# Reordering the engine programs of a two-way RWKV scan: in-chunk products behind the transitions, the decay diagonals moved, fewer filler products

## The reference, cut to what matters

```python
y = _wkv7_scan(rh, w_f, kh, vh, kk, ah)
y = y + flip(_wkv7_scan(flip(rh), flip(w_b), flip(kh), flip(vh), flip(kk), flip(ah)))
...
bonus = jnp.sum(rh * kh * r_k.astype(f32), axis=-1, keepdims=True) * vh
```

## Time and profile before

| | us |
|---|---|
| median of 3 runs | 4020.55 |
| range of the runs | 4017.84 to 4028.12 |
| the profiled execution, whole | 4013.84 |
| its span | 4012.1 |
| the scan in it (1735 to 2137 us) | 402 |
| one half turn of it, late in the scan | 22.7 |

### The profile page before, as it was taken

One profiled execution on the slowest core, in us unless ns is written; L12 is line 12 of the kernel. 1 busy time (PEld: TensorE's weight loads), 2 busy tenths in 40 slices (PEclk: granted clock), 3 DMA queues, 4 the chain that ended last, 5 costly groups with the idle time before them and its releaser, 6 DMA issues. The chain is left out here.

```text
span 4012.1 us, 63663 instructions
## 1 busy us (share of the span) xinstructions
PE 3873.1 (97%) x26819; PEld 3058.8 (76%) x26819; DVE 2264.1 (56%) x3174; ACT 1349.8 (34%) x2256; POOL 1346.7 (34%) x554
## 2 busy tenths in 40 slices
PE   8999999999999999988889999999999999999998
PEld 6866788867678887577776788778777787877886
DVE  5756567487667755567774776455550626252034
ACT  3356333243223333445553433322232111103222
POOL 1011444443234441000001444355554343654442
PEclk9999999999999999999999999999999999999999
DMA  5311222322122222531112222222212112222221
GB/s 178 129 62 41 87 105 84 111 107 108 60 84 87 101 105 106 187 118 50 46 40 87 84 105 89 89 81 84 84 63 78 62 66 87 92 105 84 87 102 63
DMA packets 43518, 359.86 MB, mean 90 GB/s; under 512 B 4323, under 2 KB 4707, under 8 KB 23948
## 3 DMA queue, kind: packets, MB, share of 16 engines
q1 hardware_dynamic: 43276, 356.35, 24.6%
HBM read 333.79 MB, written 22.28 MB: 89 GB/s over the span
## 5 line engine op out<-in xcount | busy, mean ns | idle before, releaser
L364 POOL TENSOR_TENSOR ffn_weights_low<-weight_ring,ffn_weights_high 128x2048 fp32r<-128x2048 f32 x128 | 591.7, 4622 | 785.1 <-ACT ffn_weights_high L469 784.3
L211 PE MATMUL banks<-ffn_in_high,ffn_weights_low 128*128 128x512 f32 x2048 | 800.2, 391 | 10.8 <-POOL ffn_weights_low L364 8.8
L213 PE MATMUL banks<-ffn_in_high,ffn_weights_high 128*128 128x512 f32 x2048 | 797.6, 389 | 0.0
L212 PE MATMUL banks<-ffn_in_low,ffn_weights_high 128*128 128x512 f32 x2048 | 797.4, 389 | 0.0
L211 PEld LDWEIGHTS banks<-ffn_in_high,ffn_weights_low 128*128 128x128 f32 x2048 | 384.8, 188 | 97.3 <-POOL ffn_weights_low L364 11.3
L212 PEld LDWEIGHTS banks<-ffn_in_low,ffn_weights_high 128*128 128x128 f32 x2048 | 384.9, 188 | 80.5 <-issue 0.7
L213 PEld LDWEIGHTS banks<-ffn_in_high,ffn_weights_high 128*128 128x128 f32 x2048 | 384.8, 188 | 80.0
L469 ACT ACTIVATE ffn_weights_high<-weight_ring 128x2048 fp32r<-128x2048 f32 x128 | 245.2, 1915 | 558.2 <-PE banks L213 558.2
L4034 POOL TENSOR_TENSOR third_weights_low<-weight_ring,third_weights_high 128x1024 fp32r<-128x1024 f32 x144 | 360.3, 2502 | 11.6
L623 DVE SCALAR_TENSOR_TENSOR ffn_gate<-ffn_up,columns_sb,ffn_gate 128x511 f32<-128x511 f32 (+1 forms) x132 | 273.2, 2069 | 160.7 <-ACT ffn_value L513 160.7
L4032 POOL CAST third_weights_high<-weight_ring 128x1024 fp32r<-128x1024 f32 x144 | 158.4, 1100 | 511.6 <-PE banks L213 482.7
(11 more groups left out here) (671 smaller groups left out, 7536.5 us busy)
## 6 DMA issues: line engine op xcount, KB each, us to landing
weight_ring<-weights SPq DMA_DIRECT2D x143, 2048.0 KB, 7.7
scan_in<-rwkv_operands SPq DMA_DIRECT2D x7, 1280.0 KB, 5.8
rwkv_operands<-rwin_staged SPq DMA_DIRECT2D x23, 256.0 KB, 2.2
scan_in<-rwkv_operands SPq DMA_DIRECT2D x8, 512.0 KB, 4.3
bias_tiles<-bias_rows SPq DMA_DIRECT2D x8, 448.0 KB, 8.7
residual<-x SPq DMA_DIRECT2D x4, 512.0 KB, 6.5
hyena_u_x_T<-decay SPq DMA_DIRECT2D x2, 1024.0 KB, 8.0
rwkv_residual<-residual SPq DMA_DIRECT2D x1, 2048.0 KB, 7.1
```

The lines of the kernel that those rows point to most:

```text
L211: pe.matmul(out, w[1], x[0], start=start, stop=False, skip_group_check=True)
L212: pe.matmul(out, w[0], x[1], start=False, stop=False, skip_group_check=True)
L213: return pe.matmul(out, w[0], x[0], start=False, stop=stop, skip_group_check=True)
L364: pool.tensor_tensor(parts[1], landed, parts[0].bitcast(F32), ALU.subtract).then_inc(S["split"], 1)
```

## The change

No arithmetic is added or taken away but the filler products. `within` is split into two halves (part 0 takes two of the four column groups, part 1 the other two). On PE, part 0 goes ahead of `state_step(u - 1, 1)`, right behind `transitions` and `values_carried`; part 1 behind that step. `bonus_sums` goes from behind `values_carried` to the place between `turned(u - 1, 5)` and `solved(u - 1)`. `key_rows(u + 1)` goes ahead of `carried(u, 4)`, and `past(u - 1)` behind it. The filler products go from 3 to 2 in a forward half turn, from 5 to 4 in a backward one (other counts in the first and the last), to other places: 87 become 72.

On ACT, `decay_diagonals` goes from the end of its own half turn to the start of the next pass, behind `values(u)` and ahead of `turned(u - 1, 5)`; `transitions` goes ahead of `values_carried`, and the four `decays` come earlier. On DVE, `bonus_times_value` goes ahead of `substituted`, `read` ahead of `crossed(u, 3)`, `keys` ahead of `carried(u, 3)`, `written` and `bonus_product` behind it, `past` ahead of `rows_read`, and `crossed(u, 5)` ahead of `tails`.

```diff
-            def within(u):
+            def within(u, part):
...
-                if u + 1 < HALVES:
+                if part == 0 and u + 1 < HALVES:
                     need(u + 1, "spread_done", 1)
-                for j in range(JT):
+                for j in range(part * JT // 2, (part + 1) * JT // 2):
...
-                mm.then_inc(S["own_sum"], 1)
+                if part == 1:
+                    mm.then_inc(S["own_sum"], 1)
...
                 turned(u - 1, 5)
+                bonus_sums(u)
                 if last:
                     unread(u, 1, 2)
                 solved(u - 1)
...
                 transitions(u - 1)
                 values_carried(u)
-                bonus_sums(u)
-                if u == 0 or last or u % 2 == BWD:
+                if 0 < u < HALVES and u % 2 == BWD:
+                    unread(u, 1, 2)
+                if u == 0 or last:
                     unread(u, 1, 8 if u == 0 else 3)
-                else:
-                    unread(u, 1)
+                within(u - 1, 0)
                 state_step(u - 1, 1)
-                within(u - 1)
+                within(u - 1, 1)
                 if last:
                     unread(u, 3)
                 state_step(u - 1, 2)
+                if 0 < u < HALVES:
+                    unread(u, 3)
                 turned(u, 2)
-                if last:
+                if u == 0 or last:
                     unread(u, 3)
                 state_step(u - 1, 3)
-                if u % 2 == FWD:
-                    unread(u, 3)
                 crossed(u, 3)
-                if last or u % 2 == BWD:
+                if u == 0 or last:
                     unread(u, 3)
                 state_step(u - 1, 4)
+                if 0 < u < HALVES:
+                    unread(u, 3)
                 carried(u, 3)
-                if last:
+                if u == 0 or last:
                     unread(u, 3)
                 state_step(u - 1, 5)
-                unread(u, 3)
                 turned(u, 3)
...
                 crossed(u, 4)
+                if u == 0:
+                    unread(u, 3)
+                key_rows(u + 1)
+                carried(u, 4)
                 past(u - 1)
-                carried(u, 4)
-                key_rows(u + 1)
                 turned(u, 4)
                 crossed(u, 5)
...
                 values(u)
+                decay_diagonals(u - 1)
                 turned(u - 1, 5)
                 tail_rows(u)
                 solved(u - 1)
                 factors(u)
-                values_carried(u)
-                transitions(u - 1)
                 if u >= 0:
                     decays(u + 1, 0)
+                    decays(u + 1, 1)
+                transitions(u - 1)
+                values_carried(u)
                 state_step(u - 1, 1)
                 if u >= 0:
-                    decays(u + 1, 1)
+                    decays(u + 1, 2)
+                written(u - 1)
                 state_step(u - 1, 2)
-                written(u - 1)
+                if u >= 0:
+                    decays(u + 1, 3)
                 turned(u, 2)
...
                 state_step(u - 1, 6)
-                decay_diagonals(u)
                 key_rows(u + 1)
                 turned(u, 4)
...
                 masked(u, 1)
+                bonus_times_value(u)
                 substituted(u, range(SUB - 1))
                 blocks_placed(u)
+                read(u - 1)
+                crossed(u, 3)
+                keys(u + 1)
+                carried(u, 3)
+                written(u - 1)
                 bonus_product(u + 1)
-                bonus_times_value(u)
-                written(u - 1)
-                crossed(u, 3)
-                read(u - 1)
-                carried(u, 3)
-                keys(u + 1)
                 crossed(u, 4)
                 sides(u + 1)
                 carried(u, 4)
+                past(u - 1)
                 rows_read(u + 1)
-                past(u - 1)
+                crossed(u, 5)
                 tails(u + 1)
-                crossed(u, 5)
```

More of the change, by code:

```diff
@@ L3519, in _ @@
                 factors(u)
-                values_carried(u)
-                transitions(u - 1)
                 if u >= 0:
                     decays(u + 1, 0)
+                    decays(u + 1, 1)
+                transitions(u - 1)
+                values_carried(u)
                 state_step(u - 1, 1)
                 if u >= 0:
-                    decays(u + 1, 1)
+                    decays(u + 1, 2)
+                written(u - 1)
                 state_step(u - 1, 2)
-                written(u - 1)
+                if u >= 0:
+                    decays(u + 1, 3)
                 turned(u, 2)
                 state_step(u - 1, 3)
-                if u >= 0:
-                    decays(u + 1, 2)
-                    decays(u + 1, 3)
                 state_step(u - 1, 4)
@@ L3696, in read @@
                 R = AR[:, d, :, 1, :].rearrange("p j (q t) -> p q j t", q=2)
-                if d == FWD:
-                    need(u, "own_done", 1)
+                need(u, "own_done" if d == FWD else "own_sum", 1)
                 dve.tensor_tensor(R, R, both(d)[:, :, 256:512].rearrange("p q (j t) -> p q j t", j=JT), ALU.add).then_inc(S["read_done"], 1)
```

## The result

The changed kernel takes **4031.71 us** (median; 4023.01 to 4037.55), the kernel before beside it 4019.73 (4013.11 to 4028.12). The ratio is 1.0030, with a 95% interval of 1.0022 to 1.0038: 12 us more, 9 to 15. The profiled execution of the changed kernel has a span of 4029.9 us (4031.6 in all), 17.8 more than the one of before, which lay 5.9 us under its kernel's median. So a sum made from the two traces comes out at 17.6 for the scan, and some 6 us of it belong to the two executions and not to the kernels.

What follows compares the result with a forecast made beforehand. No engine bounds the scan by its sum; handoffs between three in-order programs do. Seven forward half turns at +0.9 and eight backward at -0.2 give +4.7, with the ends +4: 4024 us, range 4009 to 4040.

Steps and rivals of the forecast that it cites:

- my own signs: Marks of a wrong forecast: forward first parts under 14 us, second part half a microsecond from 8.7, over ten half-clock stretches.
- Backward first part: Backward half turn, first grams to turning of X: 0.2 us shorter, 13.6 after 13.80, mainly from PE's first-state wait going.
- The 0.1 for splitting `within`: PE's run of `within`: splitting it breaks the overlap of its column groups once, for about 0.1 us.
- Forward, late Y: Forward half turn: eight diagonals between `values` and Y delay Y by 1.9 us and, with `tails`, all behind by 2.0.
- the rival that X ends the first part: X, not PE, ends the first part, so splitting `within` saves nothing; sum +6, 4026 us; chance 0.08.
- Forward, -1.1 regained: Forward half turn, PE from `values_carried` to turning of X: 2.28 us instead of 3.34; with late Y, first part +0.9.
- Second part: Turning of X to next first grams: about 8.7 us, taken as a change of 0, ends -0.3 and +0.3.
- The clock rival: Clock falls at the wait before `solved` in most half turns: 12 more at 1.2 us, +14, above 4038; chance 0.18.
- The waits go and nothing comes back: Rival: diagonals fit somewhere, PE's waits vanish in all parts; -15 us, 4006; chance 0.14.

Runs made afterwards that it cites:

- e2: Changed kernel with only ACT's `decay_diagonals` put back at the end of its own half turn; 4020.20 us, ratio 1.0001 to the kernel before.
- e6: Changed kernel with diagonals back at the half turn's end, `bonus_sums` back behind `values_carried`, `bonus_times_value` behind `blocks_placed`; 4009.18 us, ratio 0.9976 to the kernel before.
- e7: e6 with the filler product behind state step 5 put back, in all half turns but the first and last; 4012.28 us, ratio 0.9979 to the kernel before.
- e3: Kernel before with one edit: PE's `bonus_sums` ahead of `solved` instead of behind `values_carried`; 4017.88 us, ratio 0.9995 to the kernel before.
- e4: Changed kernel with diagonals back at the half turn's end and bonus store held until level 3 is added to X; 4019.47 us, ratio 0.9993 to the kernel before.

## Why the prediction came out as it did

I forecast 4024, +4 us, and it became +12: inside the range and on the right side, at the very edge of what I had called no change. That it lay inside is in part luck: the range reached up to 4040 for falls of the clock that did not come as I had them, and what filled it, 15 us of stops, stands in no term of the sum. Two of my own signs came out against me: the forward first part is 17.16 and not 14.9, and the forward second part, 9.61 on average, is more than half a microsecond from 8.7. By its steps:

**Backward first part: right.** I wrote 13.6; the half turns without any "issue" stop have 13.45. The wait before the first state step is gone. The 0.1 for splitting `within` does not show: at u = 13 both halves and the two state steps take 1.79 us, against 1.78 in the earlier trace rows. The means with stops fell from 14.64 to 14.11.

**Forward, late Y: right in size.** 2.40 us behind `values` as written, `solved` 1.99 later (6.26 against 4.27) where I had 2.0, and well over a microsecond of wait before it. X is placed 14.11 us behind the first grams, 2.12 later than before (I had 2.3), and never held PE in these seven half turns, so the rival that X ends the first part is out. The two runs around it bracket the price: +16 for the diagonals alone, with three falls of the clock in it, and -12 for undoing them; seven half turns at 1.9 to 2.0 are 13 to 14.

**Forward, -1.1 regained: this is the step that failed.** I took the 1.78 us of the backward half turn and 0.1 for the split, added one filler, and so let PE run from `values_carried` to the turning of X in 2.28 us. By its work it does: in half turn u = 12, from the start of `solved` to the turning, 10.15 us less the stop of 1.68 are 8.47, against 9.70 in the earlier trace rows, so 1.23 would have been regained. But the stop is there: 2.39 us on average (16.74 / 7). The first part is 17.16 and not 14.9. I took a run of PE to be as short as its products, though the earlier trace rows already showed a stop of 1.82 us that no engine caused, and I used it only for the clock. The missing row was the spacing of such stops, and the missing term is the time in which a dense run of small products can get its instructions. Moving the bonus ahead of `solved` thinned out what had covered it: with the diagonals in their old place, bonus early against bonus late is 0 against -10 us (e2, e6; the store moves with it).

**Second part: near my 0 as a change, by two errors.** The means rise by 0.27 forward and 0.08 backward, inside the ends of 0.3. But undisturbed forward second parts are 8.34 (u = 6, 10, 14), better than the 8.7 that I worked out, and the other four have half clock and 10.32 to 10.94. The waits of 0.40 before `turned`, which I had covered by "PE waits there for X anyhow", are the price of the filler that left, and they cost nothing (e7).

**In sum**, over the scans of the two traces: forward first parts +4.2 of work and late Y and +15.0 of stops (16.74 - 1.73); forward second parts +1.9; backward first parts -4.2, second +0.6; first half turn +1.0; the end -0.8. But for rounding that is the 17.6 between these two executions, of which 12 stands in the medians.

**The clock rival: its place and number were wrong, its price a little low.** Twelve more half-clock stretches were to stand at the wait before `solved`. There are four in the scan, after three, and none stands there. The stretch of the wait and the next one, in half turn u = 12 of the changed kernel:

```profile
2044.90:2048.30 3.40, 1.76 (x15) 0.96 (x18) 3.26 (x7) 3.36 (x12) 0.00 (x0) 1.00 0.00 0
2048.30:2051.70 3.40, 3.40 (x99) 3.15 (x92) 1.76 (x4) 2.23 (x6) 0.00 (x0) 1.00 0.03 5
```

PE was busy for 1.76 us of 3.40 and kept 2.4 GHz. With the diagonals moved alone there is no bonus in that wait, and it is 2.72 us long. There the clock did fall right behind it, in three of seven forward half turns (u = 8, 10, 14); u = 10:

```profile
1994.29:1997.69 3.40, 0.68 (x10) 0.47 (x8) 3.26 (x7) 3.15 (x11) 0.00 (x0) 1.00 0.00 0
1997.69:2001.09 3.40, 3.40 (x64) 3.40 (x66) 0.01 (x1) 1.88 (x4) 0.00 (x0) 0.50 0.02 5
```

That the bonus in the wait kept the clock up is what these two kernels suggest; they differ in more than the bonus, and no run isolates it. By the rule of the Trainium skill that the prediction weighed ("TensorE: Matmul & The Clock Gate", Part 4, PE-mode transpose) the stretch with the turning in it should look emptier still; it kept its clock in all seven half turns, and no run here separates transposes from products. All four stretches of the changed kernel begin in a forward second part instead, behind the stop in `within`; the first of them, with the stretch ahead of it:

```profile
1806.33:1809.73 3.40, 2.10 (x58) 1.72 (x58) 0.69 (x1) 1.41 (x4) 0.00 (x0) 1.00 0.00 0
1809.73:1813.13 3.40, 2.93 (x45) 2.27 (x45) 2.00 (x4) 0.50 (x3) 0.00 (x0) 0.50 0.02 5
```

These second parts are 2.0 to 2.6 us longer than the 8.34 of the others. The 2.6 belong to u = 2, where the half clock lasts for 6.83 us, twice as long as in the others. Less the other stops and waits that stand in them alone ("issue" 0.57 and 0.53, ACT's state 0.74), the other three cost 1.3 to 1.6 each; I had priced a stretch at 1.2. The link between stop and clock is seen, not isolated: the three half turns without a fall had stops of 2.70, 2.75 and 1.72 too.

**"The waits go and nothing comes back"** failed in its condition, ACT's order, as argued. Without the diagonals' move and the bonus's, the rest of the change does give 10 us, of the 15 that this rival had named.

**Open:** what passes in the 1.1 to 1.6 us between the end of a packet and PE's next instruction, which instruction asks for the next block, and whether a stop brings down the clock behind it. No run here tried it.

## What to carry to other kernels

Work that nobody needs yet must not be placed in an in-order engine's list between a late input and the copy that another engine waits for, even when that engine is idle for most of the time: look on which side of the wait the idle time lies. Before filling or removing a wait of PE in a run of small products, look for "issue" stops in its timeline and count all of PE's instructions between them, waits included; where they lie on a grid, removed waits and removed work can come back as stops. In such a run, independent work in a few large products was free here (e6), and was better kept there than moved into a wait elsewhere.

## What the hardware showed

PE's program arrives in blocks, and a dense run of small fp32 products is faster than they come. Each of these products counts as two instructions, weight load and product; 256 of PE's instructions go with one packet of 16 KB (84 packets in the scan for 84.0 such blocks), and at the long stops PE stood for 0.98 to 3.08 us and went on 1.1 to 1.6 us after the packet had ended. The Trainium skill, in "Runtime: NRT & Kernel Launch", section "Instruction fetch mechanics", says that instructions are refilled in blocks of 16 KiB, 256 instructions, and that the cost of crossing a border is mostly hidden. The traces agree on the block (187 packets, 3.06 MB; stops on a grid of 256) and on most borders, and differ on the cost in such a run: it is hidden where PE waits for something else anyhow, as in e3, and 16.74 us in the seven forward half turns of the changed kernel. In the run from one border to the next, 2.1 to 2.2 us of products took 3.23 us or more (e4). Where other transfers filled the DMA engines to 76 to 82%, the packet began 2.05 to 2.78 us behind the last border; with those transfers moved away it began at 1.04 to 1.71 us, and up to 1.65 us came off a stop.
